# Where the causal mask of a prompt's attention is added: identity products on TensorE, or one addition in PSUM on VectorE

## What is computed

```python
s = jnp.einsum('bqhd,bshd->bhqs', qb, k).astype(jnp.float32) * scale + cb[..., :, None] - c[..., None, :]
qpos = start + jnp.arange(Q_BLOCK)
p = _masked_softmax(s, (kpos[None, :] <= qpos[:, None])[None, None])
return jnp.einsum('bhqs,bshd->bqhd', p.astype(v.dtype), v)
```

## Time and profile before

| | |
|---|---|
| median of three runs | 1419.85 us (1419.55, 1419.85, 1425.75) |
| the profiled execution | 1424.95 us |
| its span | 1423.2 us |
| TensorE, matmuls | 1204.9 us busy, 85% of the span |
| TensorE, weight loads | 813.7 us, 57% |
| VectorE | 802.0 us, 56% |
| ScalarE | 228.5 us, 16% |
| DMA | 282 MB, 198 GB/s on the mean |

### The profile page before, as it was taken

One profiled execution on the slowest core, in us unless ns is written; L12 is line 12 of the kernel. 1 busy time (PEld: TensorE's weight loads), 2 busy tenths in 40 slices (PEclk: granted clock), 3 DMA queues, 4 the chain that ended last, 5 costly groups with the idle time before them and its releaser, 6 DMA issues. The chain is left out here.

```text
span 1423.2 us, 27444 instructions
## 1 busy us (share of the span) xinstructions
PE 1204.9 (85%) x10100; PEld 813.7 (57%) x10100; DVE 802.0 (56%) x1167; ACT 228.5 (16%) x692; POOL 173.1 (12%) x149
## 2 busy tenths in 40 slices
PE   0656677999999577999999888989899799999996
PEld 0655566887888455544444466766556364665542
DVE  1444331298989973335544547676776948544123
ACT  0010041112121111233333410110000000000023
POOL 0000000120000000000000073144051422410000
PEclk9978879999999775699999999999999989998998
DMA  8898524267888632187767194466578767657620
GB/s 221 248 314 240 169 85 148 89 222 217 277 280 295 213 78 75 49 306 226 258 233 233 60 291 152 149 193 229 160 231 260 248 209 234 221 176 270 244 93 31
DMA packets 205900, 282.01 MB, mean 198 GB/s; under 512 B 21749, under 2 KB 126734, under 8 KB 205254
## 3 DMA queue, kind: packets, MB, share of 16 engines
q1 hardware_dynamic: 109958, 202.40, 43.0%
q10 hardware_dynamic: 89376, 60.01, 14.8%
q0 software_dynamic: 6432, 17.83, 3.8%
HBM read 273.26 MB, written 11.11 MB: 200 GB/s over the span
## 5 line engine op out<-in xcount | busy, mean ns | idle before, releaser
L1735 PE MATMUL bank<-xnT,e_wg 128*128 128x260 f32 x1152 | 282.9, 405 | 0.0
L1735 PEld LDWEIGHTS bank<-xnT,e_wg 128*128 128x128 f32 x1152 | 230.8, 203 | 54.5 <-issue 15.8
L585 PE MATMUL score_banks<-xnT,oT 128*128 128x260 f32 (+1 forms) x864 | 196.8, 386 | 8.4 <-DMA oT<-in_w_in 8.4
L1719 POOL DMA_INDIRECT d_slc<-in_cache_nsa_slc,selrow x128 | 154.8, 1210 | 273.5 <-PE score_banks L1811 234.1
L585 PEld LDWEIGHTS score_banks<-xnT,oT 128*128 128x128 f32 (+1 forms) x864 | 161.3, 189 | 38.4 <-DMA oT<-in_w_in 8.7
L249 PE MATMUL score_banks<-c_cols,c_w 64*64 64x64 f32 (+1 forms) x4096 | 97.2, 256 | 96.6 <-issue 58.3
L249 PEld LDWEIGHTS score_banks<-c_cols,c_w 64*64 64x64 f32 x4096 | 92.4, 168 | 101.2 <-issue 101.2
L299 DVE COPY c_cols<-oT 128x1024 f32<-128x1024 f32 x48 | 49.6, 1159 | 92.5 <-DMA oT<-in_cache_nsa_cmp 67.1
L1398 DVE TENSOR_REDUCE f_pt<-score_banks 128x2 f32<-128x512 f32 (+3 forms) x56 | 45.1, 805 | 80.0 <-PE score_banks L1319 78.0
L1743 PE MATMUL bank<-oT,e_wb 128*128 128x512 f32 x192 | 89.0, 607 | 0.0
L1363 PE MATMUL bank<-mt,rpast 128*8 128x512 f32 x320 | 59.9, 601 | 6.1 <-DMA mt<-in_cache_fox_kv 5.0
(11 more groups left out here) (390 smaller groups left out, 1447.1 us busy)
## 6 DMA issues: line engine op xcount, KB each, us to landing
mt<-in_cache_fox_kv SPq DMA_DIRECT2D x240, 256.0 KB, 3.8
d_kpage<-in_cache_fox_kv SPq DMA_DIRECT2D x96, 256.0 KB, 4.4
d_vpage<-in_cache_fox_kv SPq DMA_DIRECT2D x96, 256.0 KB, 3.6
oT<-in_cache_fox_kv SPq DMA_DIRECT2D x80, 256.0 KB, 3.8
e_wg<-in_w_in ACTq DMA_DIRECT2D x36, 512.0 KB, 5.1
oT<-in_cache_nsa_cmp SPq DMA_DIRECT2D x128, 128.0 KB, 3.8
oT<-in_w_in ACTq DMA_DIRECT2D x13, 1024.0 KB, 6.9
oT<-in_cache_nsa_cmp ACTq DMA_DIRECT2D x64, 128.0 KB, 3.7
```

The costliest lines, as they stand in the source:

```text
L585: last = nc.tensor.matmul(pj[ch.n % 2][i][0:ch.w, 0:NM if ch.mem else TH], w[:, c, ch.off:ch.off + ch.w], rhs, start=c == 0, stop=c == DC - 1)
L1719: nc.gpsimd.indirect_dma_start(out=slc[:, b % 2, n, :], out_offset=None, in_=k.cache_slc, in_offset=bass.IndirectOffsetOnAxis(ap=k.selrow[ ...
L1735: last = nc.tensor.matmul(gate_bank[n % 2][:, 0:TH], wg[product % WR][:, c, :], k.xnT[:, c, part * TH:(part + 1) * TH], start=c == 0, stop ...
```

## The change

For every unit with a mask the two identity products are left out. VectorE now adds the mask itself, in place, in PSUM: one `tensor_tensor` over 128 partitions, two banks and the last 128 columns of each, before `tensor_reduce` takes the maximum over all columns. The addition raises a new semaphore, `masked`, and VectorE waits for it, so that the maximum reads what was written. The count it waits for, `u.masks`, is the number of units with a mask so far. The forget sums are added by products as before; the last product on each bank now closes it.

```diff
+    for u in units:
+        u.masks = sum(v.kind != "mem" for v in units[:u.no + 1])
...
+        masked = sem("f_masked")
...
+        own_block = lambda u: k.score_banks[:, 2 * (u.no % 2):2 * (u.no % 2) + 2, u.t * P:u.n]
...
-                    more = u.kind != "mem"
+                    more = u.kind == "fox"
...
                     if u.kind == "fox":
                         for j in range(2):
-                            nc.tensor.matmul(score(u)[j][:, 0:u.n], k.ident[0:H, 2 * u.c + j:2 * u.c + j + 1].to_broadcast([H, P]),
-                                             k.ncum[:, 0:u.n], start=False, stop=False, skip_group_check=True)
-                    if more:
-                        for j in range(2):
-                            last = nc.tensor.matmul(score(u)[j][:, u.t * P:u.n], k.ident, k.causal, start=False, stop=True,
-                                                    skip_group_check=True)
+                            last = nc.tensor.matmul(score(u)[j][:, 0:u.n], k.ident[0:H, 2 * u.c + j:2 * u.c + j + 1].to_broadcast([H, P]),
+                                                    k.ncum[:, 0:u.n], start=False, stop=True, skip_group_check=True)
...
                 def maximum(u):
                     ve.wait_ge(s_done, u.no + 1)
+                    if u.kind != "mem":
+                        nc.vector.tensor_tensor(own_block(u), own_block(u), k.causal.unsqueeze(1).to_broadcast([P, 2, P]), ALU.add).then_inc(masked, 1)
+                        ve.wait_ge(masked, u.masks)
                     nc.vector.tensor_reduce(nm[:, u.no, :], both(u), AX, ALU.max, negate=True).then_inc(m_done, 1)
```

## The result

The changed kernel takes 1414.24 us (median of 14 runs), the kernel before, beside it on the same chips, 1422.75. The ratio is 0.9938, with a 95% interval of 0.9913 to 0.9964: 8.8 us faster. The forecast was 14.6 us. The sign was right, and the time lies in the range, 0.8 us from its upper end, but the size was much too large. (The ratios leave out executions in a slower state of the chip; the medians have them in.) The profiled run took 1418.39 us, its span 1416.6 against 1423.2.

A forecast was written before the change was run, and what follows sets the result against it. TensorE and the page stream through a ring of eight were taken as bounds from 600 us on. Gains of 4.1 (half clock), 3.2 (forget sets) and 7.3 (slc and win) sum to 14.6 us, giving 1405 us, range 1388 to 1415.

The forecast's parts named there:

- The price of a mask step: Prompt's attention on TensorE: removing a unit's two identity products saves 0.64 us at full clock, 1.07 on the mean at half.
- B: Page group before the turn of t = 1 in a four-unit set; forecast 2.40 us after the set's first group, formerly 3.04.
- Half clock and forget sets: Stage's early units: seven half-clock masks save 4.1 us; of nine full-clock forget masks five count, 3.2 us.
- the exchange by 0.6: Stage start: with 40 us of half clock staying, time saved there is worth 0.64/1.07 = 0.6 of its length.
- Slc and win sets: Eight sets at full clock, 32 masks: page landings limit the gain to 7.3 us.
- the walk through the ring: Following value pages through the eight-slot ring, landings taken as fixed, set by set; gave the slc and win sets 7.3 us.
- D: Page group before the turn of t = 3 in a four-unit set; its end forecast to stay 11.93 us after the first group.
- the sets with a fold: Among the slc and win sets, those where a fold replaces a late page group; forecast 1.3 to 1.4 us gained each.
- rival 2: Page stream takes all of the slc and win gain, clock dips a little more; about 5 us gained, 1415 us; chance 22%.
- The addition beside other work: VectorE's 48 mask additions, 0.45 us each with the wait: 22 us, hidden beside TensorE's work and late pages.
- Rival 1: Slc and win sets not pinned: pages land sooner and all masks count, 31.6 us gained, some 1388 us; chance 14%.
- rival 3: Stage's half clock lasts longer, each us costing 0.4 to 0.45; slower, some 1426 us with a rise at 640; chance 6%.

The follow-up runs named there:

- e6: Changed kernel without the VectorE addition, so no mask at all; ratio 0.9904 to the kernel before, median 1410.94 us.
- e17: Changed kernel with ScalarE's page sums ahead of the exponentials, a second timing of the same program; ratio 0.9876 to the kernel before, median 1404.67 us.
- e11: Kernel before, with ScalarE's page sums moved ahead of the exponentials; ratio 0.9953 to the kernel before, median 1418.50 us.
- e10: Changed kernel with ScalarE's page sums moved ahead of the exponentials; ratio 0.9864 to the kernel before, median 1399.50 us.
- e5: Kernel before with all identity products kept and VectorE's mask addition on top; ratio 1.0027 to the kernel before, median 1430.38 us.
- e7: Changed kernel with the eight 511 KB window-state copies issued after the last page; ratio 0.9922 to the kernel before, median 1411.05 us.
- e2: Changed kernel loading only the first eight value pages; ratio 0.9731 to the kernel before, median 1385.49 us.
- e4: Changed kernel with VectorE adding masks in slc and win units only, forget units keeping their products; ratio 0.9978 to the kernel before, median 1420.96 us.
- e8: Changed kernel with the five folds issued behind the unit's turn; ratio 0.9927 to the kernel before, median 1413.97 us.
- e1: Kernel before, loading only the first eight value pages; ratio 0.9872 to the kernel before, median 1404.54 us.
- e3: Changed kernel with VectorE adding masks in the 16 forget units only, the others keeping their products; ratio 0.9949 to the kernel before, median 1416.88 us.
- e12: Changed kernel with two idle TensorE products ahead of each fold and each first page group behind one; ratio 0.9959 to the kernel before, median 1417.57 us.
- e15: Changed kernel with page sums first on ScalarE and only the first eight pages loaded; ratio 0.9678 to the kernel before, median 1380.34 us.
- e13: Changed kernel with page sums first on ScalarE and the window-state copies issued after the last page; ratio 0.9872 to the kernel before, median 1406.55 us.
- e16: Changed kernel with VectorE adding masks in forget units only and page sums first on ScalarE; ratio 0.9907 to the kernel before, median 1411.97 us.
- e14: Kernel before with page sums first on ScalarE and only the first eight pages loaded; ratio 0.9810 to the kernel before, median 1398.83 us.

## Why the prediction was right or wrong

**The price of a mask step** (0.64 us from start to start, not the busy time) was right: B came at 2.40 as worked out, and the weight-load rule of the Trainium skill (Perfetto Trace Analysis, Identifying the Most-Contended Engine), by which TensorE would have had room to spare, was rightly set aside; removing the products did move the time, by 13.7 us in e6.

**Half clock and forget sets.** Forecast 4.1 and 3.2, measured 6.6 and 2.7 in the first two pieces. The two must be read together, since the first piece is at half clock throughout and what the exchange by 0.6 takes back would come behind it: 7.3 forecast, 9.3 measured. The stall at the turn of unit 2 was there (0.66 us at 573.90, for 0.7). That half of the masks turn into page waits was right: between the page groups at 599.65 and 639.38 before, 595.92 and 633.14 after, all at full clock, eight masks gain 2.5 us, which is four of them. What failed is that the clock would rise at the same moment. It did 35.7 us behind the first scores instead of 41.2, and 5.5 us less of half clock, at some 0.4 us each, are the 2 us beyond the forecast. That is no property of the change: in the 18 profiles of this study the half clock at the start of the stage ended 26 to 41 us behind the first scores, with the products and without. Here the gain was luck, and the term can only be given as some 4 to 7 us.

**Slc and win sets: the step that failed.** Forecast 7.3, measured 1.3 in the third piece. Two things in it were wrong. First, the walk through the ring took the landings as fixed to A: B as free of the ring, D's string as starting 5.34 behind A, D's end as staying at 11.93. B's own second pair came late (the row of 2.03 us), D's string started 6.36 behind A, and D's end came at 12.97. The mask between D's end and the next A was won (5.87 before, 5.22 after), and the 1.04 that D was late ate it. So a plain set gains nothing, not 0.64; all four of them together take 74.1 us in both kernels, and e17 and e11 say nearly the same without folds in the way. Second, the sets with a fold were to gain about 1.4 each, since TensorE's longer pause there was balanced by the mask ahead. The balance was right (A to the fold 6.67 us before and 6.51 after, 0.16 less for the 0.64 - 0.45 = 0.19 counted), but the pauses of 1.9 and 2.0 us were followed by 7 us of half clock each, 6.8 us of full speed together against 1.7 before. This stood in rival 2 as "a dip or two" of 1 to 2 us, and not in the sum. With the pauses gone (e10, e17, against e11) three of these sets gain 4.7 to 4.9 us together. A third part was no fault of the reasoning: the half clock from 634.5 us, 3.4 us, without a pause ahead. The same chance helped at the start of the stage and hurt here.

**The addition beside other work.** Its length was right, its cover mostly: 4 to 5 us for 21 us of work, where 2 were counted. The fold's pause, whose path holds the addition, is longer by it (0.47 us, e5 and e6 above), and the half clock behind it may be the rest; the times are too uncertain to show it.

**The rivals.** Rival 2 was the nearest in mechanism: the slc and win sets gained next to nothing and the clock dipped more often. Its gain of 5 us is 3.8 short of the measured one; that its 1415 stands so near the 1414.24 is luck, since the kernel before came out 2.9 us slower than the three runs from which that was reckoned. The Trainium skill's rule (Perfetto Trace Analysis, What "DMA-bound" means) named the issuing queue as the bound; the strings in the set above, one 2.14 us behind the other in both kernels, agree with it, e7 does not bear it out as far as the queue's other traffic goes, and e2 shows the stream as a whole worth some 11 us to the change. Rival 1 and rival 3 did not come about; the clock did not stay low.

## What to carry to other kernels

Before work is taken from the busiest engine, look at where it already pauses: what is removed ahead of a pause only lengthens it, and on TensorE a pause of 2 us went with 4 to 10 us of half clock, so most of a saving can be lost again. Then look at what the pause waits for and move that: here one change of order on ScalarE was worth 6.7 us alone, and with the change of this document 1.3% of the run. When following a ring of buffers, go once round the whole ring before holding any of its steps as free or its landings as fixed. And when a stage owes microseconds to the clock, compare several profiles: one pair of them can differ by as much without a cause in the program.

## What the runs showed of the hardware

The granted clock fell at or behind every pause of 1.94 to 2.05 us that TensorE made at a fold or at the first page group behind one: nine pauses, two in the changed kernel, e2, e4 and e7 each and one in e8, with 4 to 10 us of half clock. Of twelve shorter ones at the same places (0.93 to 1.58 us, in before, e1, e3, e5, e6, e8 and e12) seven were followed by it. Page waits of 1.87 us in before and 1.73 in the changed kernel were followed by it, one of 2.19 in e10 was not, nor one of 1.72 for VectorE in e15 (at 763.32 us, the clock at 1.00 to 770).

It also fell without a pause. Between 607 and 645 us nine of the 18 profiles (the changed kernel, e1, e3, e4, e5, e8, e11, e13, e16) have a stretch of 4 to 10 us of half clock with no idle piece above 0.1 us in the 10 us ahead of it; the other nine have none there. So the fall is tied to pauses of 2 us, but not by their length alone and not to them alone; what else decides was not settled.

The lasting rise of the clock came 26 to 41 us behind the first scores of this stage, with and without the products, and 31 and 28 us in e14 and e15, 41 and 36 in the kernel before and the changed one, whose programs are the same as theirs up to there; in e4, e5 and e11 it had been at full speed for 3 us at 568 and fell again. Two single profiles can therefore differ by some 6 us in the first part of this stage for no reason in the program, and the pieces given above carry that uncertainty.

An addition with both its first input and its output in PSUM, over 128 partitions of 256 elements, took 0.43 us, about as long as a maximum over as many (0.42).
